# Two decoder blocks on one core: the first two split tiles behind each norm taken pair by pair, and a few steps of the mixers in another order

## Chip, cores and metric

The kernel runs on one NeuronCore of a Trainium2 chip. The metric is the device time of one execution in microseconds (us), taken as the median of several executions; lower is better. A difference of 0.2% (6.1 us) is about what can be told from no change.

## What is computed

An input x of 256 tokens and 1024 channels passes through two blocks. Cut to what matters:

```python
def first_block(x, ...):
    for i in range(2):
        h = rms_norm(x, norm_g[i, 0]) * (1.0 + sc1) + sh1
        x = x + g1 * (hgrn2_mixer(h, ...) if i % 2 == 0 else rglru_mixer(h, ...))
        h = rms_norm(x, norm_g[i, 1]) * (1.0 + sc2) + sh2
        x = x + g2 * peer_ffn(h, peer_w_q[i], ...)          # q = h @ w_q, then 16384 experts
    return rms_norm(x, final_g)

def second_block(x, ...):
    h = x
    for layer in range(2):
        mix = even_mixer(h, ...) if layer % 2 == 0 else odd_mixer(h, ...)   # start with h @ w_in
        h = layer_norm(ALPHA * h + mix, ...)
        ffn = conv_ffn(h, ffn_w_up[layer], ...)                             # starts with h @ w_up
        h = layer_norm(ALPHA * h + ffn, ...)
    return h
```

`even_mixer` runs a gated delta rule over 6 heads beside a dilated attention; `odd_mixer` runs a differential attention beside gated linear attention (GLA, `gla_chunked`), whose two normed outputs go through `w_out`. All is float32.

## The kernel before, in words

Activations are held transposed: 8 chunks of 128 channels by 256 tokens. Weights come as one long stream of tiles of 128x1024 (512 KB) through a ring of four buffers in SBUF, loaded by the queue of SyncE in the order of use. For most of them a product in full float32 is replaced by three passes in float32r: ScalarE rounds a tile to `w_high` (`split_high`, L1205, in two halves of 128x512), VectorE subtracts to get `w_low` (`split_low`, L2229, two halves too), and TensorE adds h_high*w_low, h_low*w_high and h_high*w_high (`passes`, L535 to L537). `w_high` and `w_low` have room for two tiles. A tile gives one chunk of 128 output channels and takes 8 input chunks, so 24 matmuls of 256 columns; its sums stand in one of four slots of PSUM (`product_slot`), and semaphores count its first half (`mid_tile`), its whole (`tile_done`) and the reading out of its slot (`product_taken`).

Each engine has its own program, and the order of work is written out by hand; only the choice of experts follows a table made ahead. Six of these products stand right behind a norm, so that their input is made while TensorE waits: `wq0` and `wq1` (queries of the two expert layers, behind an RMS norm with modulation), `even_in`, `up0`, `odd_in` and `up1`. There VectorE first scales the eight chunks by the inverse root (L1887, L1890), then ScalarE applies gain and shift twice for each chunk (`affine`: L1308 writes the rounded `h_high`, L1309 the whole value), and for each pair of chunks VectorE subtracts (`split_pair`, L1895), which makes `h_low` and raises `h_split` by one. So the input comes in four pairs of chunks. TensorE runs 12 idle matmuls of constants (`stay_busy`, L601: float32, so that each stands as two in the trace), waits for pair 0, takes its 6 matmuls of the first tile, runs 2 idle matmuls, waits for pair 1, and so on; from the second tile on nothing is waited for but weights:

```python
for q in range(4):
    m = 4 * b + q
    if fresh is not None and m % 2 == 0:
        stay_busy(busy[m // 2])
        pe.wait_ge(sem("h_split"), fresh[m // 2])
    ins = passes(dst, k, b, q, ...)
```

In `even_mixer` small steps stand between the 42 tiles of `even_in`, each behind tile j: `mixing` (L843, 12 columns at a time) behind 0, `beta_rows` (L853) behind 3, 5 idle matmuls and `gam_columns` (L862) behind 4, `gam_row` (L873) behind 5 to 7, attention from 9 on, and at the end 6 idle matmuls and `gdn_squares(0)` (L652) behind 38, `gdn_values` (L935) behind 39, `gdn_squares(1)` behind 40. ScalarE reads out tile j, rounds tile j + 2 and then does its small steps: the rows of beta (L1532) at j = 4, SiLU of q and k (L1549) and v (L1551) and the squares (L1265) at j = 36 to 38. In `odd_mixer` the projection of the gate (L1101, then L1108) stands behind tiles 0 and 1. GLA begins with transposes of v (L693), which ScalarE copies out (L1337) behind three other steps (squares, SiLU, rounding of two tiles); TensorE's second set of scores (L718) waits for that copy behind 8 idle matmuls.

Of the kernel before, what the change touches and what calls it, by code (L numbers as in the profile page):

```python
# [26 lines left out]
T = 256  # L27
# [173 lines left out]
def build(nc, tiles, ada_in, x_in, params_in, consts_in, small_in, masks_in, lam_in, bias_in, skew, out):  # L201
# [5 lines left out]
    with ctx:  # L207
# [277 lines left out]
        def _(pe):  # L485
# [65 lines left out]

# [6 lines left out]
            NORMED, MIXED = (12, 2, 2, 2), (0, 0, 0, 0)  # L558

            def split_linear(name, order=(0, 1, 2, 3), busy=MIXED):  # L560
# [4 lines left out]
                def body(k, it):  # L565
                    pe.wait_ge(taken, it * 4 + (q0 + k - 3))
                    split_product(product_slot(q0 + k), s0 + k, it, 4, h0 if k == 0 else None, busy)

                spans(pe, body, (0, 1, n) if any(busy) else (0, n))
# [175 lines left out]
            def peer(layer):  # L745
                split_linear(f"wq{layer}", busy=NORMED)
# [85 lines left out]
            def even_mixer():  # L832
# [105 lines left out]
                for j in range(n):  # L938
                    pe.wait_ge(taken, q0 + j - 3)
                    split_product(product_slot(q0 + j), s0 + j, 0, 4, h0 if j == 0 else None, NORMED)  # L940
# [115 lines left out]
            def odd_mixer():  # L1056
# [39 lines left out]
                for j in range(n):  # L1096
                    pe.wait_ge(taken, q0 + j - 3)
                    split_product(product_slot(q0 + j), s0 + j, 0, 4, h0 if j == 0 else None, NORMED)
# [6 lines left out]
                    if j == 1:  # L1105
# [85 lines left out]
        def _(act):  # L1191
# [84 lines left out]
            def rms(name=None, run=None):  # L1276
                if name in SUMS:
                    copy_sums(name)
                for i in range(DC // 2):
# [303 lines left out]
            def odd_mixer():  # L1583
# [53 lines left out]
                act.wait_ge(sem("diff_out_taken"), 4 * TT)  # L1637
                squares(e["mix"][:, 0:4 * T], e["sq"][:, 0:4 * T], "head_squares")
# [1249 lines left out]
```

## Time and profile before

| | us |
|---|---|
| median of 3 executions | 3068.2 (3067.02 to 3068.53) |
| the profiled execution, its own time | 3065.36 |
| its span in the profile | 3063.6 |
| TensorE, matmuls | 2980.6 busy (97%) |
| TensorE, weight loads | 2720.8 busy (89%) |
| VectorE | 2234.2 busy (73%) |
| ScalarE | 1633.2 busy (53%) |
| GpSimd | 62.1 busy (2%) |
| mean granted TensorE clock | 0.991 of full speed |

PE is TensorE's matmul side, PEld its weight loads, DVE is VectorE, ACT ScalarE, POOL GpSimd, SP SyncE. An engine is busy while one of its instructions executes; matmuls are pipelined, so that one stands with about 280 ns where the next starts 118 ns later. Idle matmuls of `stay_busy` count as busy.

### The profile page before, as it was taken

To read this page: it belongs to the slowest core of one execution; us is meant where nothing else is said; L and a number is where in the kernel's file an instruction comes from. 1 tells how busy PE (TensorE), PEld (TensorE's weight loads), DVE (VectorE), ACT (ScalarE), POOL (GpSimd) and SP (SyncE) were. 2 spreads that over 40 slices of the span, in tenths; PEclk is the share of its full clock that TensorE was granted. 3 is DMA by queue.
4 is the path that set the end of the run, shared out by engine and by line. 5 is a ranking of instruction groups with operands and counts; after the bars stand their busy time and mean duration, and the time that the engine had idled before them with its cause. 6 is when DMAs were issued, how large, how long until landed. Compare 5 with 4: busy or idle time off the path is not lost.

```text
span 3063.6 us, 58305 instructions
## 1 busy us (share of the span) xinstructions
PE 2980.6 (97%) x19920; PEld 2720.8 (89%) x19920; DVE 2234.2 (73%) x4764; ACT 1633.2 (53%) x3372; POOL 62.1 (2%) x112
## 2 busy tenths in 40 slices
PE   7998999999999999999999999999999999999998
PEld 6888899999987778889999988888898999888996
DVE  5336499888779985649898877777486678765786
ACT  1112557778644443655777854444555258463674
POOL 3000000000001100000000000000000000000000
PEclk8999999999999999999999999999999999999999
DMA  9521455444468863445444445555442145432453
GB/s 389 193 89 40 140 186 166 152 162 142 157 241 308 309 212 112 156 145 186 163 155 159 145 162 188 188 189 187 140 138 83 38 165 177 160 119 89 148 175 117
DMA packets 137692, 503.14 MB, mean 164 GB/s; under 512 B 15312, under 2 KB 15440, under 8 KB 137264
## 3 DMA queue, kind: packets, MB, share of 16 engines
q1 hardware_dynamic: 122544, 445.63, 43.2%
q0 software_dynamic: 14976, 55.19, 5.0%
q8 instruction: 112, 1.84, 0.2%
q14 instruction: 60, 0.49, 0.0%
HBM read 498.65 MB, written 2.10 MB: 163 GB/s over the span
## 4 chain that ended last, share of the span: by engine, by line
PE 81%; DVE 5%; ACT 4%; issue 1%; DVEq 0%; ACTq 0%
PE PB L535 14%; PE PB L536 14%; PE PB L537 13%; PE PA L581 9%; PE PA L582 9%; PE PA L580 8%; PE PA L777 4%; PE PB L525 2%; DVE w_low L2229 2%; PE PA L992 1%; PE PA L1165 1%; PE PA L631 1%; PE PB L601 1%; DVE BIG L2255 1%; ACT h_high L1308 1%
## 5 line engine op out<-in xcount | busy, mean ns | idle before, releaser
L1205 ACT ACTIVATE w_high<-ring 128x512 fp32r<-128x512 f32 x1548 | 962.2, 630 | 847.6 <-PE PA L582 466.4
L2229 DVE TENSOR_TENSOR w_low<-ring,w_high 128x512 fp32r<-128x512 f32 x1548 | 1051.0, 691 | 429.7 <-ACT w_high L1205 414.1
L535 PE MATMUL PB<-h_high,w_low 128*128 128x256 f32 x3792 | 1083.8, 286 | 15.2 <-DVE h_low L1895 6.2
L536 PE MATMUL PB<-h_low,w_high 128*128 128x256 f32 x3792 | 1067.9, 282 | 0.0
L537 PE MATMUL PB<-h_high,w_high 128*128 128x256 f32 x3792 | 1066.1, 281 | 0.0
L535 PEld LDWEIGHTS PB<-h_high,w_low 128*128 128x128 f32 x3792 | 721.4, 190 | 32.4 <-DVE h_low L1895 14.7
L536 PEld LDWEIGHTS PB<-h_low,w_high 128*128 128x128 f32 x3792 | 715.6, 189 | 0.2
L537 PEld LDWEIGHTS PB<-h_high,w_high 128*128 128x128 f32 x3792 | 714.5, 188 | 0.0
L581 PE MATMUL PA<-w_high,a_low 128*128 128x512 f32 x1200 | 476.3, 397 | 0.0
L580 PE MATMUL PA<-w_low,a_high 128*128 128x512 f32 x1200 | 470.4, 392 | 4.3 <-DVE a_low L2238 3.6
L582 PE MATMUL PA<-w_high,a_high 128*128 128x512 f32 x1200 | 474.0, 395 | 0.0
L580 PEld LDWEIGHTS PA<-w_low,a_high 128*128 128x128 f32 x1200 | 225.4, 188 | 68.9 <-issue 8.2
L581 PEld LDWEIGHTS PA<-w_high,a_low 128*128 128x128 f32 x1200 | 224.9, 187 | 53.0
L582 PEld LDWEIGHTS PA<-w_high,a_high 128*128 128x128 f32 x1200 | 225.2, 188 | 49.4
L525 PE MATMUL PB<-H,ring 128*128 128x256 f32 x896 | 198.3, 384 | 1.7 <-ACT H L1309 1.7
L525 PEld LDWEIGHTS PB<-H,ring 128*128 128x128 f32 x896 | 173.0, 193 | 26.0 <-issue 1.8
L777 PE MATMUL PA<-onehot_b,onehot_a 128*128 128x128 f32 x1024 | 137.5, 277 | 2.9 <-issue 2.6
L2238 DVE TENSOR_TENSOR a_low<-BIG,a_high 128x256 fp32r<-128x256 f32 x300 | 127.7, 426 | 10.3
L777 PEld LDWEIGHTS PA<-onehot_b,onehot_a 128*128 128x128 f32 x1024 | 124.8, 191 | 6.7 <-issue 3.3
L1855 DVE SCALAR_TENSOR_TENSOR BIG<-BIG,coef 128x1024 f32<-128x1024 f32 (+1 forms) x80 | 102.5, 1282 | 16.8 <-DMA BIG<-ada 15.2
L1411 ACT ACTIVATE onehot_a<-inv,slots 128x128 f32<-128x128 f32 x256 | 110.9, 481 | 0.0
L2255 DVE SCALAR_TENSOR_TENSOR BIG<-PB,par,BIG 128x255 f32 (+3 forms) x176 | 84.5, 480 | 14.8 <-DVE BIG L2255 14.5
(334 smaller groups left out, 2704.1 us busy)
## 6 DMA issues: line engine op xcount, KB each, us to landing
ring<-tiles SPq DMA_DIRECT2D x842, 512.0 KB, 3.3
BIG<-ada POOLq DMA_DIRECT2D x96, 512.0 KB, 6.6
BIG<-skew POOLq DMA_DIRECT2D x4, 512.0 KB, 5.0
X<-x SPq DMA_DIRECT2D x1, 1024.0 KB, 5.8
skew<-BIG POOLq DMA_DIRECT2D x1, 1024.0 KB, 6.3
out<-X SPq DMA_DIRECT2D x4, 256.0 KB, 2.1
con<-consts SPq DMA_DIRECT2D x1, 911.0 KB, 8.8
BIG<-masks POOLq DMA_DIRECT2D x1, 768.0 KB, 6.7
```

The source lines that it names most:

```text
L525: ins = mm(product_slot(q0 + i), wt[:, k * P:(k + 1) * P], src[:, k * T:(k + 1) * T], start=k == 0, stop=k == DC - 1)
L535: mm(dst, lhs_l, high, start=start, stop=False, skip_group_check=True)
L536: mm(dst, lhs_h, low, start=False, stop=False, skip_group_check=True)
L537: return mm(dst, lhs_h, high, start=False, stop=stop, skip_group_check=True)
L580: mm(dst, high[:, own], w_l, start=first, stop=False, skip_group_check=True)
L581: mm(dst, low[:, own], w_h, start=False, stop=False, skip_group_check=True)
L582: ins = mm(dst, high[:, own], w_h, start=False, stop=last, skip_group_check=True)
L777: ins = mm(PA[:, (g % 4 * 4 + i) * P:(g % 4 * 4 + i + 1) * P], onehot_a[:, i * P:(i + 1) * P], onehot_b[:, i * P:(i + 1) * P], start=True, ...
L1205: fn(tile_half(w_high, s, b), ring[:, at:at + HALF], ACT.Identity).then_inc(sem("high_ready"), 1)
L2229: tt(tile_half(w_low, s, b), ring[:, at:at + HALF], tile_half(w_high, s, b).bitcast(F32), ALU.subtract).then_inc(sem("low_ready"), 1)
L2238: tt(pair(a_low, j), a, pair(a_high, j).bitcast(F32), ALU.subtract)\
L2255: stt(dst, product_slot(q0 + j)[:, 0:T - sh], wt[tap][:, bass.ds(it * 4 + j, 1)], dst, ALU.mult, ALU.add).then_inc((taken, sem("conv_step" ...
```

## The change

Behind each of the six norms the first two tiles are taken together by a new function, `fresh_two`: 12 idle matmuls, then for each pair of input chunks 6 matmuls of tile 0 and 6 of tile 1, in two PSUM slots. There are no idle matmuls between the pairs. `even_in`, `up0`, `odd_in` and `up1` go side by side; `wq0` and `wq1` take tile 1 one pair later. So that tile 1's weights are there in time, VectorE makes its `w_low` between pairs 1 and 2 in `wq0` and `wq1`, and in `even_in` both engines split tile 1 ahead of the norm.

```diff
-            def split_product(dst, k, it, step, fresh=None, busy=(0, 0, 0, 0)):
+            def split_product(dst, k, it, step, fresh=None):
...
-                            stay_busy(busy[m // 2])
...
+            SIDE_BY_SIDE = [(i, part) for part in range(DC // 2) for i in range(2)]
+            ONE_LATER = [(0, 0), (0, 1), (1, 0), (1, 1), (0, 2), (1, 2), (0, 3), (1, 3)]
+
+            def fresh_two(q, k, fresh, busy, sequence):
+
+                for i in range(2):
+                    if q + i >= 4:
+                        pe.wait_ge(taken, q + i - 3)
+                stay_busy(busy)
+                for i, part in sequence:
+                    b = part // 2
+                    if part % 2 == 0:
+                        pe.wait_ge(sem("low_ready"), 2 * (k + i) + b + 1)
+                    pe.wait_ge(sem("h_split"), fresh[part])
+                    for m in (2 * part, 2 * part + 1):
+                        ins = passes(product_slot(q + i), k + i, b, m % 4, h_high[:, m * T:(m + 1) * T],
+                                     h_low[:, m * T:(m + 1) * T], m == 0, m == DC - 1)
+                    if part % 2:
+                        ins.then_inc((sem("mid_tile"), tile_done)[b], 1)
...
-            NORMED, MIXED = (12, 2, 2, 2), (0, 0, 0, 0)
+            NORMED = 12
...
-                spans(pe, body, (0, 1, n) if any(busy) else (0, n))
+                if sequence:
+                    fresh_two(q0, s0, h0, NORMED, sequence)
+                spans(pe, body, (2, n) if sequence else (0, n))
...
-                split_linear(f"wq{layer}", busy=NORMED)
+                split_linear(f"wq{layer}", sequence=ONE_LATER)
...
-                split_linear(f"up{i}", busy=NORMED)
+                split_linear(f"up{i}", sequence=SIDE_BY_SIDE)
```

The rest moves steps. `mixing` and the gate's first product now stand behind tiles 0 and 1, the gate's second product behind tile 2 in place of tile 1, `gam_columns` behind tile 5 in place of tile 4 and without its 5 idle matmuls (VectorE's part moves with it), `gdn_values` behind tile 38 with 4 idle matmuls in place of 6, and `gdn_squares(0)` behind tile 39. In GLA ScalarE copies v out first:

```diff
-                    if j == 4:
-                        stay_busy(5, IDLE_EVEN)
+                    if j == 5:
                         gam_columns()
...
                     if j == n - 4:
                         pe.wait_ge(sem("attention_out_taken"), 4 * TT)
-                        stay_busy(6, IDLE_EVEN)
+                        stay_busy(4, IDLE_EVEN)
+                        gdn_values()
+                    if j == n - 3:
                         gdn_squares(0)
-                    if j == n - 3:
-                        gdn_values()
...
-            def decay_attention(cfg):
+            def decay_attention(cfg, beside=None):
                 n = cfg["heads"] * T
                 act.wait_ge(sem("decay_vt_psum"), w.up(sem("decay_vt_psum")))
                 fn(cfg["vt"], PA[:, 0:n], ACT.Identity).then_inc(sem("decay_vt_ready"), 1)
+                if beside is not None:
+                    beside()
...
                 if run is not None:
-                    split_whole(dst, "whole_ready")
-                    split_low(run, 1)
+                    for i in range(DC // 2):
+                        split_pair(dst, "whole_ready", i)
+                        if i == 1:
+                            split_low(run, 1)
```

TensorE at the head of `up0`, before: the idle matmuls (L601), the first pair of tile 0 (L535 to L537), the wait for the second. `w_low` and `w_high` are the halves of the weight tile, `h_high` and `h_low` of the input.

```order
L601 MATMUL PB<-con 128x256 x11
L535 MATMUL PB<-h_high,w_low 128x256 [waits h_split]
L536 MATMUL PB<-h_low,w_high 128x256
L537 MATMUL PB<-h_high,w_high 128x256
L535 MATMUL PB<-h_high,w_low 128x256
L536 MATMUL PB<-h_low,w_high 128x256
L537 MATMUL PB<-h_high,w_high 128x256
L601 MATMUL PB<-con 128x256 x2
L535 MATMUL PB<-h_high,w_low 128x256 [waits h_split]
```

And now, from the second chunk of tile 0 on:

```order
L535 MATMUL PB<-h_high,w_low 128x256
L536 MATMUL PB<-h_low,w_high 128x256
L537 MATMUL PB<-h_high,w_high 128x256
L535 MATMUL PB<-h_high,w_low 128x256 [waits h_split,low_ready]
L536 MATMUL PB<-h_low,w_high 128x256
L537 MATMUL PB<-h_high,w_high 128x256
L535 MATMUL PB<-h_high,w_low 128x256
L536 MATMUL PB<-h_low,w_high 128x256
L537 MATMUL PB<-h_high,w_high 128x256
L535 MATMUL PB<-h_high,w_low 128x256 [waits h_split]
```

Where the idle matmuls stood, the same pair is now taken with tile 1's weights, and the wait for the next pair stands behind 12 matmuls and not 6.

VectorE at the head of `wq0`, before (L1890 scales, L1895 makes `h_low` of a pair, L2229 `w_low` of half a tile):

```order
L1890 TENSOR_TENSOR BIG<-X,inv 128x512 [waits dve_step]
L1890 TENSOR_TENSOR BIG<-X,inv 128x512 x3
L1895 TENSOR_TENSOR h_low<-BIG,h_high 128x512 [waits whole_ready] x4
L2229 TENSOR_TENSOR w_low<-ring,w_high 128x512 [waits high_ready] x2
L183 UNCONDITIONAL_BRANCH
```

And now (32 to 34 lines further down in the file):

```order
L1922 TENSOR_TENSOR BIG<-X,inv 128x512 [waits dve_step]
L1922 TENSOR_TENSOR BIG<-X,inv 128x512 x3
L1927 TENSOR_TENSOR h_low<-BIG,h_high 128x512 [waits whole_ready] x2
L2263 TENSOR_TENSOR w_low<-ring,w_high 128x512 [waits high_ready] x2
L1927 TENSOR_TENSOR h_low<-BIG,h_high 128x512 [waits whole_ready] x2
```

Tile 1's two halves moved ahead of the last two pairs.

TensorE in `even_in` behind tile 4, before (L862 is `gam_columns`, and the last row starts tile 5):

```order
L537 MATMUL PB<-h_high,w_high 128x256
L601 MATMUL PA<-con 128x256 x5
L862 MATMUL PA<-BIG,con 128x6 [waits g_ready,beta_rows_taken]
L862 MATMUL PA<-BIG,con 128x6 x2
L535 MATMUL PB<-h_high,w_low 128x256 [waits low_ready,product_taken]
```

And now, behind tile 5 (L883 is `gam_columns`, L894 a `gam_row`, the last row starts tile 6):

```order
L537 MATMUL PB<-h_high,w_high 128x256
L883 MATMUL PA<-BIG,con 128x6 [waits g_ready,beta_rows_taken]
L883 MATMUL PA<-BIG,con 128x6 x2
L894 MATMUL PA<-con,BIG 128x128 x6
L535 MATMUL PB<-h_high,w_low 128x256 [waits low_ready,product_taken]
```

The idle matmuls are gone, and a whole tile stands between `beta_rows` being sent to ScalarE and the wait for its copy.

## Rows read from the trace of the kernel before

**Rows 1.** The page's first part: busy us of each engine.

```profile
PE 2980.6 (97%) x19920; PEld 2720.8 (89%) x19920; DVE 2234.2 (73%) x4764; ACT 1633.2 (53%) x3372; POOL 62.1 (2%) x112
```

**Rows 2.** Timeline, head of up0: start us, us, engine, line [idle before <-releaser].

```profile
2471.58 0.39 PE L535 MATMUL PB<-h_high,w_low 128*128 128x256 f32 x1 [0.80 <-DVE h_low L1895]
...
2472.39 1.02 PE L601 MATMUL PB<-con 128*128 128x256 f32 x4
...
2472.80 0.69 DVE L1895 TENSOR_TENSOR h_low<-X,h_high 128x512 fp32r<-128x512 f32 x1 [1.27 <-ACT X L1309]
...
2477.48 0.38 PE L535 MATMUL PB<-h_high,w_low 128*128 128x256 f32 x1
2477.94 0.28 PE L535 MATMUL PB<-h_high,w_low 128*128 128x256 f32 x1
2478.29 0.28 PE L535 MATMUL PB<-h_high,w_low 128*128 128x256 f32 x1
```

**Rows 3.** Timeline, head of wq0, in all engines.

```profile
317.69 0.62 ACT L1205 ACTIVATE w_high<-ring 128x512 fp32r<-128x512 f32 x1
...
322.67 0.38 PE L535 MATMUL PB<-h_high,w_low 128*128 128x256 f32 x1 [0.73 <-DVE h_low L1895]
...
323.89 0.69 DVE L1895 TENSOR_TENSOR h_low<-BIG,h_high 128x512 fp32r<-128x512 f32 x1 [1.27 <-ACT BIG L1309]
...
328.43 2.51 DVE L2229 TENSOR_TENSOR w_low<-ring,w_high 128x512 fp32r<-128x512 f32 x4
```

**Rows 4.** TensorE's idle before two rows (timeline), in hg_out and even_mixer.

```profile
289.46 0.36 PE L535 MATMUL PB<-h_high,w_low 128*128 128x256 f32 x1 [1.84 <-DVE BIG L1951]
...
2350.91 1.56 PE L601 MATMUL PB<-con 128*128 128x256 f32 x6 [1.63 <-ACT BIG L1508]
```

**Rows 5.** Stretches: us, PE busy (x), granted clock as a share, DMA share, GB/s.

```profile
290.60:294.00 3.40, 3.40 (x19) 0.51 0.03 7
...
2351.00:2354.00 3.00, 3.00 (x14) 1.00 0.00 0
2185.00:2188.30 3.30, 3.30 (x18) 0.51 0.78 273
```

**Rows 6.** Timeline, head of even_in.

```profile
2175.17 0.47 PE L535 MATMUL PB<-h_high,w_low 128*128 128x256 f32 x1
...
2175.68 0.69 DVE L1895 TENSOR_TENSOR h_low<-X,h_high 128x512 fp32r<-128x512 f32 x1 [0.91 <-ACT X L1309]
...
2180.77 3.64 PE L843 MATMUL PA<-SM,X 128*128 128x12 f32 x32
...
2184.26 0.36 PE L535 MATMUL PB<-h_high,w_low 128*128 128x256 f32 x1
```

**Rows 7.** Timeline, even_in behind tile 4.

```profile
2199.87 2.32 PE L601 MATMUL PA<-con 128*128 128x256 f32 x10
...
2201.39 1.44 ACT L1532 ACTIVATE BIG<-PA 128x1536 f32<-128x1536 f32 x1
...
2202.88 0.83 PE L862 MATMUL PA<-BIG,con 128*128 128x6 f32 x6 [0.69 <-ACT BIG L1532]
2203.57 0.37 PE L535 MATMUL PB<-h_high,w_low 128*128 128x256 f32 x1
```

**Rows 8.** Timeline, even_in behind tile 38.

```profile
2330.68 2.75 PE L601 MATMUL PA<-con 128*128 128x256 f32 x12
...
2331.14 1.48 ACT L1551 ACTIVATE BIG<-BIG 128x1536 f32<-128x1536 f32 x1
...
2334.04 2.86 PE L652 MATMUL PA<-BIG,con 128*128 128x256 f32 x12 [0.61 <-ACT BIG L1265]
...
2336.55 0.47 PE L535 MATMUL PB<-h_high,w_low 128*128 128x256 f32 x1
```

**Rows 9.** Timeline, start of GLA in odd_mixer.

```profile
2773.80 3.72 PE L601 MATMUL PA<-con 128*128 128x256 f32 x16
...
2777.88 1.26 PE L718 MATMUL PA<-BIG 64*128 64x128 f32 x16 [0.36 <-ACT BIG L1337]
```

More of the change, by code:

```diff
@@ L556, in fresh_pairs, with split_linear @@
                 return [h0 + order.index(i) + 1 for i in range(DC // 2)]
-            NORMED, MIXED = (12, 2, 2, 2), (0, 0, 0, 0)
-            def split_linear(name, order=(0, 1, 2, 3), busy=MIXED):
+            NORMED = 12
+            def split_linear(name, order=(0, 1, 2, 3), sequence=None):
                 s0, (q0, n) = SPLIT_AT[name][0], product_at[name]
@@ L566, in body @@
                     pe.wait_ge(taken, it * 4 + (q0 + k - 3))
-                    split_product(product_slot(q0 + k), s0 + k, it, 4, h0 if k == 0 else None, busy)
-                spans(pe, body, (0, 1, n) if any(busy) else (0, n))
+                    split_product(product_slot(q0 + k), s0 + k, it, 4, h0 if k == 0 else None)
+                if sequence:
+                    fresh_two(q0, s0, h0, NORMED, sequence)
+                spans(pe, body, (2, n) if sequence else (0, n))
             def split_sums(j, k, it, step, first=False, last=False):
@@ L938, in even_mixer @@
                 for j in range(n):
-                    pe.wait_ge(taken, q0 + j - 3)
-                    split_product(product_slot(q0 + j), s0 + j, 0, 4, h0 if j == 0 else None, NORMED)
+                    if j == 0:
+                        fresh_two(q0, s0, h0, NORMED, SIDE_BY_SIDE)
+                    if j >= 2:
+                        pe.wait_ge(taken, q0 + j - 3)
+                        split_product(product_slot(q0 + j), s0 + j, 0, 4)
                     if j == 0:
@@ L1096, in odd_mixer @@
                 for j in range(n):
-                    pe.wait_ge(taken, q0 + j - 3)
-                    split_product(product_slot(q0 + j), s0 + j, 0, 4, h0 if j == 0 else None, NORMED)
+                    if j == 0:
+                        fresh_two(q0, s0, h0, NORMED, SIDE_BY_SIDE)
+                    if j >= 2:
+                        pe.wait_ge(taken, q0 + j - 3)
+                        split_product(product_slot(q0 + j), s0 + j, 0, 4)
                     if j == 0:
@@ L1104, in odd_mixer @@
                         ins.then_inc(sem("gate_psum"), 1)
-                    if j == 1:
+                    if j == 2:
                         pe.wait_ge(sem("gd_ready"), w.up(sem("gd_ready")))
@@ L1274, in copy_sums, with rms @@
                 fn(TMP[:, 0:D], PA[:, 0:D], ACT.Identity).then_inc(sem("sums_copied"), 1)
-            def rms(name=None, run=None):
+            def rms(name=None, run=None, early=None):
                 if name in SUMS:
                     copy_sums(name)
+                if early is not None:
+                    split_high(early, 1)
                 for i in range(DC // 2):
@@ L1636, in odd_mixer, with beside @@
                             .then_inc(sem("gla_gate_ready"), 1)
-                act.wait_ge(sem("diff_out_taken"), 4 * TT)
-                squares(e["mix"][:, 0:4 * T], e["sq"][:, 0:4 * T], "head_squares")
-                act.wait_ge(taken, q0 + n)
-                fn(e["r"], e["r"], ACT.Silu).then_inc(sem("gate_silu"), 1)
-                split_high("odd_out", 0)
-                split_high("odd_out", 1)
-                decay_attention(GLA)
+                def beside():
+                    act.wait_ge(sem("diff_out_taken"), 4 * TT)
+                    squares(e["mix"][:, 0:4 * T], e["sq"][:, 0:4 * T], "head_squares")
+                    act.wait_ge(taken, q0 + n)
+                    fn(e["r"], e["r"], ACT.Silu).then_inc(sem("gate_silu"), 1)
+                    split_high("odd_out", 0)
+                    split_high("odd_out", 1)
+                decay_attention(GLA, beside)
                 decayed_squares(e["sq"][:, 4 * T:8 * T], GLA_HEADS)
@@ L1727, in _ @@
             split_high("even_in", 0)
-            rms("experts1")
-            split_high("even_in", 1)
+            rms("experts1", early="even_in")
             affine(X, p("final_g"), None, "x_out", split=True)
@@ L2384, in even_mixer @@
                         gates()
-                    if j == 4:
+                    if j == 5:
                         gam_columns()
@@ L2674, in _ @@
             split_low("even_in", 0)
+            split_low("even_in", 1)
             rms("experts1", X)
             split_x()
-            split_low("even_in", 1)
             even_mixer()
```

## Prediction, made before the changed kernel was run

> **What bounds the kernel now.** I read the page's first part, then the timelines of the places that the change touches, then the granted clock of single stretches. TensorE is busy for 2980.6 of 3063.6 us and VectorE for 2234.2 [rows 1]: TensorE sets the pace, and what is taken out of its program shortens the run, if the others can follow. But busy counts idle matmuls too, so the page hides the time in question. The head of `up0` shows it [rows 2]. Pair 0 starts at 2471.58 and the last of the four at 2477.48, 5.90 us later: a pair comes every 1.97 us. Its 6 matmuls need 0.81 us (0.46 for the first chunk behind float32 work, then 0.35 for each chunk); 1.02 us more are idle matmuls, and then TensorE waits. What it waits for is made by ScalarE: VectorE sat idle for 1.27 us before `h_low`, released by ScalarE's L1309. So ScalarE sets 1.97 us for a pair, and TensorE uses two fifths of it. Meanwhile tile 1 is ready and waits for its turn. The same pattern stands in `wq0` [rows 3], `wq1`, `odd_in` and `up1`, with 1.96 to 1.97 us for a pair in each.
>
> **The change part by part.**
>
> *Five heads of this pattern.* A chunk costs 0.353 us (2477.94 to 2478.29), a tile of 8 chunks 2.82 us. Before, from the start of the last pair to the end of tile 1: 0.81 + 2.82 = 3.63 us. Now only the last pair of both tiles is left: 0.81 + 0.71 = 1.52 us. The gain is 2.11 us, the six chunks of tile 1 that now lie in the waits. Two pairs of work (1.52) fit in 1.97 us. The six idle matmuls that go cost nothing: they lay in the waits. In `wq0` and `wq1` VectorE has to put tile 1's two halves between pairs 1 and 2. Four halves took 2.51 us, so two take 1.25, and its gap there is 1.27 us [rows 3]: it fits with nothing to spare, and if it did not, pairs 2 and 3 would come some 0.1 us late. ScalarE has rounded tile 1 before pair 0 [rows 3]. Taking tile 1 one pair later leaves TensorE a gap of 1.97 - 0.81 = 1.16 us behind pair 0; then three pairs of work (0.81 + 0.71 + 0.71 = 2.23 us) run 0.26 us into pair 2, whose 1.41 us end before pair 3. What follows is late for nothing: tile 2 needs its first `w_low` half 1.5 us behind the last pair, and VectorE has that much less to do there, since tile 1 is behind it; its second half waits for tile 0's end, which stays where it was. Each head is worth 2.11 us, five are worth 10.6. In `odd_in` the gate's two products are moved and not changed. Bounds for one head: 0 if the waits only move to tile 2, 2.4 at most.
>
> *Head of `even_in`.* Here TensorE comes late: it starts pair 0 at 2175.17, while the last `h_low` is done at 2176.4 [rows 6]. So all pairs are ready, and the six idle matmuls are paid for. Before, tile 0 and its idle matmuls took 5.60 us (to 2180.77). Now both tiles take 16 chunks, 5.65 us, and 0.19 for the slow first one: 5.84. `mixing` (3.49 us) follows, and tile 2 starts 0.24 us behind the point where tile 1 started. A tile of 2.82 + 0.10 is gone, for 0.24: 2.7 us. The two splits moved ahead of the norm lie beside adds and squares, and TensorE has 12 idle matmuls of cover behind them; if they delayed the norm by their 1.3 us, pair 0 would still be there in time. Behind `mixing` the clock is 0.51 for 3.3 us [rows 5]. Its place behind `mixing` stays, so I leave this cost (1.65 us) as it is: it would now fall on tile 2.
>
> *`gam_columns`.* From the end of tile 4 to tile 5 it took 3.70 us (2199.87 to 2203.57): 2.32 idle matmuls, 0.69 waiting for ScalarE's copy of the beta rows, 0.69 its own [rows 7]. The copy ended at 2202.83, 2.96 us behind tile 4. Tile 5 now covers 2.82 of that, so 0.2 us of wait and the 0.69 stay: 2.8 us gained. VectorE's part moves with it; the rows of decay that follow it are needed a tile later, and ScalarE's next rounding (tile 7) stands behind the copy, 4 us before TensorE needs it. Bounds: 0 (the wait moves to the first `gam_row`) and 3.0.
>
> *Tail of `even_in`.* Before, 3.36 us passed from 2330.68 to the start of the squares, with 0.61 idle for ScalarE. The transposes of v need only its SiLU, done at 2331.14 + 1.48 = 2332.62, and the 4 idle matmuls end at 2332.5 [rows 8]. So they start 2.0 us behind tile 38, and the squares find their input done a tile later. The root that follows still waits for the last squares. Gain 1.4 us; bounds 0.5 (the two idle matmuls alone) and 1.5.
>
> *GLA.* The scores waited 0.36 us more than their 3.72 us of idle matmuls [rows 9]. The copy comes out 3 us earlier, the idle matmuls stay: 0.4 us. What ScalarE did before the copy has the whole of the scores' loop as cover. Bounds 0 and 0.4, since nothing shortens the idle matmuls.
>
> Sum: 10.6 + 2.7 + 2.8 + 1.4 + 0.4 = 17.9 us. The profiled execution's 3065.4 would become 3047.5; the median lies 2.8 us above it, so 3068.2 - 17.9 = **3050.3 us**.
>
> **Weighed against a rule.** The idle matmuls keep the clock. After 1.84 us without a matmul in `hg_out` [rows 4] the granted clock was 0.51, 1.2 GHz, from 290.6 for 3.4 us; after 1.63 us it stayed at 1.00, 2.4 GHz [rows 4, 5]. In `wq0` the new gaps are 0.73 and 1.16 us with 0.81 us of work between, 1.89 together, just in the range where it fell. The Trainium skill, TensorE: Matmul & The Clock Gate, section "Why this matters for your kernels", tells one only to avoid idle gaps of over about 3 us. By that rule no gap here matters and the sum stays 17.9 us; by the rows it can fall, and the trace differs from the rule, since 1.84 us were enough.
>
> **The rivals.**
>
> *The clock falls in `wq0` or `wq1`.* For it: the rows above. Against: two gaps are not one, and in the other four heads the gap between pairs is only 0.45 us, less than the waits that the clock stands now. Price: from pair 1 on there are 14 chunks, which end 5.5 us later. With 3.4 us at half clock, 4.8 chunks are done there and 9.2 (3.2 us) left: 6.6 us, so 1.2 lost. One head gives 3051.5, both 3052.7 us.
>
> *`even_in` gives back what it gains at `gam_columns`.* There ScalarE and VectorE work in a fixed order, and copy, columns and decay rows now come closer together. For it: ScalarE's copy already ended last [rows 7]. Without the 2.8 us: 3053.1 us; without the tail's 1.4 as well, 3054.5.
>
> *The slow stretch behind `mixing` goes.* 48 dense matmuls stand before it now. 1.7 us less: 3048.6 us.
>
> *The change doesn't do what it says.* Two tiles in turn, each with its own slot, could run slower than one, or the waits could all come back at tiles 2 and 3. Without the 10.6 and the 2.7 us: 3063.6 us. Against it: the weights of all tiles are ready well ahead in the trace, and each chunk loads new weights anyway.
>
> *Slower.* The idle matmuls between pairs go in all six heads. If the clock fell there and stayed down, each 3.4 us at half costs 1.7 us where TensorE doesn't wait. The point from which it decides is 17.9 / 1.7, 11 such stretches. At three for each head, 18 x 1.7 = 30.6 us, it would be 3080.9 us. Against it: between pairs TensorE works 1.52 of 1.97 us.
>
> **How the numbers follow.** Forecast 50%, clock 25%, `even_in` 13%, slow stretch gone 5%, not as it says 5%, slower 2%. The likeliest is 3050.3 us. The range takes in the first four cases, with 1.5 us for the runs' own spread at the lower end: 3047.0 to 3055.0 us. Only the last two cases and some tails lie outside. Faster by over 0.2% (6.1 us, about what a measurement can tell): 0.93; within 0.2%: 0.05; slower: 0.02.
>
> **What would show it.** Right: in `up0` four starts of a pair 1.97 us apart, 12 matmuls behind each, tile 2 about 1.5 us behind the last; in `wq0` VectorE's L1895, L1895, two `w_low` and L1895 with no delay of the third; in `even_in` tile 2 starting at the distance at which tile 1 did, no idle before `gam_columns` over 0.3 us, and `gdn_values` 2.0 us behind tile 38. Wrong: a clock of 0.5 in any of the six heads, idle time of TensorE at tiles 2 or 3 released by `w_low`, or a wait for the decay rows behind tile 6. A gain of under 13 us would mean that one of the larger terms failed.

## The result, and the profile after

| | before | changed |
|---|---|---|
| median, us | 3067.6 (3065.0 to 3068.5, 4 executions) | 3049.2 (3048.1 to 3050.1, 4 executions) |
| ratio, 95% interval | | 0.9941 (0.9924 to 0.9958) |
| span of the profiled execution | 3063.6 | 3048.4 |
| mean granted clock of TensorE | 0.991 | 0.990 |

The change makes the kernel 18.4 us faster by the medians; the interval of the ratio allows 13 to 23. The forecast was 3050.3 us. A later set of five executions (e4 below) gave 3048.0 against 3065.5 for the kernel before on the same chip, 17.5 us less. TensorE's line of the page, which answers to [rows 1], hardly shows it: its busy time fell by 14.4 us, with 86 matmuls fewer, and it is still at 97%.

```profile
PE 2966.2 (97%) x19834; PEld 2712.9 (89%) x19834; DVE 2232.6 (73%) x4764; ACT 1631.9 (54%) x3372; POOL 62.3 (2%) x112
```

So one has to read distances. The table takes, in each trace, the distance in us between two steps of TensorE that both kernels have: from the squares ahead of a norm to the next step named. e4 is the changed kernel, profiled a second time.

| stretch of TensorE | before | changed | e4 | gain | forecast |
|---|---|---|---|---|---|
| wq0: squares to the first step of the experts | 58.19 | 57.20 | 56.08 | 0.99, in e4 2.11 | 2.11 |
| wq1: the same | 58.27 | 56.17 | 56.17 | 2.10 | 2.11 |
| even_in: squares to `mixing` | 18.48 | 18.73 | 18.73 | -0.25 | -0.24 |
| even_in: `mixing` to the first `gam_row` | 25.72 | 20.02 | 19.98 | 5.70 | 5.7 |
| from there to the squares ahead of up0 | 255.39 | 254.02 | 254.06 | 1.37 | 1.4 |
| up0, to the next squares | 212.27 | 210.13 | 210.71 | 2.14, in e4 1.56 | 2.11 |
| odd_in with its mixer and GLA | 162.51 | 159.76 | 159.76 | 2.75 | 2.5 |
| up1, to the next squares | 213.57 | 211.41 | 211.46 | 2.16 | 2.11 |

(The forecast's 2.7 us for the head of even_in are the -0.24 and 2.92 of the 5.7.) The changed column adds up to 17.0 us, e4's to 17.5. Why up0 gave 0.6 less in e4: most of it begins at 2479.82, where TensorE waits 0.27 us for a half of `w_low`: VectorE took 1.8 us for each of two halves beside steps of GpSimd, and takes 0.69 for one elsewhere. That GpSimd is the cause isn't shown.

The span fell by 15.2 only, because the code that both share didn't take the same time in the two executions: from the first squares of the program to those of wq0 it took 301.8 us in place of 299.9 (in the other profiles below 299.7 to 302.0). Slow stretches, in which the granted clock is at its lower level, stand in other places too: the one of before at 382.8 is absent, and others stand at 217.8 and 1371.5. In the same way 1.4 of the 18.4 us by which the medians differ stand in no row of the table. That is why the runs spread over 3 us, and why single terms are read from distances and not from spans.

Timeline of the changed kernel, head of `up0` (start us, us, engine, line, [idle before <-releaser]); it answers to [rows 2]:

```profile
2463.54 0.36 PE L535 MATMUL PB<-h_high,w_low 128*128 128x256 f32 x1 [0.90 <-DVE h_low L1927]
...
2464.67 0.69 DVE L1927 TENSOR_TENSOR h_low<-X,h_high 128x512 fp32r<-128x512 f32 x1 [1.27 <-ACT X L1337]
2465.42 0.39 PE L535 MATMUL PB<-h_high,w_low 128*128 128x256 f32 x1 [0.22 <-DVE h_low L1927]
...
2467.48 0.36 PE L535 MATMUL PB<-h_high,w_low 128*128 128x256 f32 x1 [0.38 <-DVE h_low L1927]
...
2469.36 0.39 PE L535 MATMUL PB<-h_high,w_low 128*128 128x256 f32 x1 [0.23 <-DVE h_low L1927]
```

The pairs still come 1.9 to 2.1 us apart (2463.54, 2465.42, 2467.48, 2469.36), and VectorE still waits 1.27 us for ScalarE's whole value. But between them stand four chunks of work, and TensorE waits only 0.2 to 0.4 us.

The same view of VectorE in `wq0` answers to [rows 3]. The columns are the same.

```profile
325.82 0.69 DVE L1927 TENSOR_TENSOR h_low<-BIG,h_high 128x512 fp32r<-128x512 f32 x1 [1.28 <-ACT BIG L1337]
326.43 1.29 DVE L2263 TENSOR_TENSOR w_low<-ring,w_high 128x512 fp32r<-128x512 f32 x2
327.80 0.69 DVE L1927 TENSOR_TENSOR h_low<-BIG,h_high 128x512 fp32r<-128x512 f32 x1
329.76 0.69 DVE L1927 TENSOR_TENSOR h_low<-BIG,h_high 128x512 fp32r<-128x512 f32 x1 [1.27 <-ACT BIG L1337]
```

The two halves of tile 1 fill the gap exactly: pair 2 comes at 327.80, 1.98 us behind pair 1, and pair 3 again 1.96 later. TensorE and its granted clock (stretch, us, PE busy, clock as a share, DMA share, GB/s) in `wq0`, `wq1` and behind `mixing`:

```profile
324.70:326.50 1.80, 0.94 (x6) 1.00 0.00 0
326.90:330.30 3.40, 3.40 (x19) 0.52 0.40 131
1316.40:1319.80 3.40, 3.39 (x29) 1.00 0.44 134
2183.20:2186.60 3.40, 3.40 (x20) 0.60 0.94 340
```

In `wq0` the granted clock is 0.52 over 3.4 us, which is its lower level of 1.2 GHz for all but the start, behind two waits of 0.82 and 0.92 us with 0.9 us of work between them: 19 matmuls in 3.4 us. In `wq1`, the same program with waits of 0.91 and 0.93 us, it stayed at 1.00 (2.4 GHz), with 29. The slow stretch behind `mixing` is there as before [rows 5]. The move of `gam_columns` and the tail of even_in answer to [rows 7] and [rows 8]:

```profile
2197.53 1.45 ACT L1562 ACTIVATE BIG<-PA 128x1536 f32<-128x1536 f32 x1
2199.03 0.83 PE L883 MATMUL PA<-BIG,con 128*128 128x6 f32 x6
...
2323.96 1.89 PE L622 MATMUL PA<-con 128*128 128x256 f32 x8
2324.43 1.48 ACT L1581 ACTIVATE BIG<-BIG 128x1536 f32<-128x1536 f32 x1
2325.96 1.53 PE L956 MATMUL PA<-con,BIG 128*128 128x128 f32 x12
```

ScalarE's copy ends at 2198.98, while tile 5 runs, and `gam_columns` follows with no wait. `gdn_values` starts 2.0 us behind tile 38. In GLA the second set of scores follows its idle matmuls directly (2764.86, where it waited 0.36 us [rows 9]).

### The profile page after: what moved, and what is told of

The parts are those of the page before. It is cut to its first block, busy times and chain, and to the rows that moved or that the text cites. A ratio compares the mean times of both kernels' runs of the same rounds, so it can differ in the third digit from the quotient of the medians.

```text
span 3048.4 us, 58151 instructions
## 1 busy us (share of the span) xinstructions
PE 2966.2 (97%) x19834; PEld 2712.9 (89%) x19834; DVE 2232.6 (73%) x4764; ACT 1631.9 (54%) x3372; POOL 62.3 (2%) x112
## 4 chain that ended last, share of the span: by engine, by line
PE 81%; DVE 5%; ACT 3%; issue 1%; DVEq 0%; ACTq 0%
PE PB L535 14%; PE PB L536 14%; PE PB L537 13%; PE PA L602 9%; PE PA L603 9%; PE PA L601 9%; PE PA L798 4%; PE PB L525 2%; DVE w_low L2263 2%; PE PA L1015 1%; PE PA L1191 1%; PE PA L652 1%; DVE BIG L2289 1%; PE PB L622 1%; ACT h_high L1336 1%
## 5 line engine op out<-in xcount | busy, mean ns | idle before, releaser
L535 PE MATMUL PB<-h_high,w_low 128*128 128x256 f32 x3792 | 1084.1, 286 | 18.1 <-DVE h_low L1927 11.0
L537 PE MATMUL PB<-h_high,w_high 128*128 128x256 f32 x3792 | 1067.7, 282 | 0.0
L535 PEld LDWEIGHTS PB<-h_high,w_low 128*128 128x128 f32 x3792 | 723.2, 191 | 31.1 <-issue 15.7
L537 PEld LDWEIGHTS PB<-h_high,w_high 128*128 128x128 f32 x3792 | 716.1, 189 | 0.0
L601 PE MATMUL PA<-w_low,a_high 128*128 128x512 f32 x1200 | 471.4, 393 | 4.3 <-DVE a_low L2272 3.5
L601 PEld LDWEIGHTS PA<-w_low,a_high 128*128 128x128 f32 x1200 | 226.0, 188 | 68.8 <-issue 8.2
```

What stands on the lines that cost most here:

```text
L535: mm(dst, lhs_l, high, start=start, stop=False, skip_group_check=True)
L537: return mm(dst, lhs_h, high, start=False, stop=stop, skip_group_check=True)
L601: mm(dst, high[:, own], w_l, start=first, stop=False, skip_group_check=True)
```

## Experiments

Each was timed in four or five executions (e1 in eleven), beside the kernel before on the same chip: its median was 3065.5 us beside e1 to e4, 3067.2 beside e5 to e8, 3067.0 beside e9 to e11 and 3065.8 beside e12. e4 was timed beside the first of these, so that differences to e4 in e5 to e12 hold the difference between chips too; where it matters, the gain over each one's own before is given beside them. Medians of the same kernel differ by up to 1.7 us here. So for a term of a few us the distances in the trace decide, and the time only bounds it.

**e4, the changed kernel again.** No edit.

> The changed kernel unchanged, as the base of the three others on the same chip and as a second look at wq0. Theory (the fall of the clock in wq0 comes from its two gaps of 0.8 and 0.9 us and is there in each execution): 3049.2 us, and again a stretch near 0.5 behind pair 1 of wq0, none in wq1. Rival (chance of where in time the gaps fall): the fall is absent here, or stands in wq1.

Measured: 3048.0 us, ratio 0.9941 (0.9927 to 0.9954). The same head of `wq0`, with the same waits, at full clock:

```profile
322.88 0.36 PE L535 MATMUL PB<-h_high,w_low 128*128 128x256 f32 x1 [0.83 <-DVE h_low L1927]
324.75 0.39 PE L535 MATMUL PB<-h_high,w_low 128*128 128x256 f32 x1 [0.93 <-DVE h_low L1927]
```

```profile
325.10:328.50 3.40, 3.40 (x30) 1.00 0.42 139
```

The distance of wq0 is 56.08 us, 1.12 less than with the fall. The fall is therefore no fixed property of this program: the rival holds in that it was absent. That it is chance isn't shown by this; e11 comes back to it. The price of the fall is 1.12 us.

**e1, the kernel before without the idle matmuls between pairs.** This asks whether the gain is in taking tile 1 along, or in the idle matmuls that went.

```diff
-            NORMED, MIXED = (12, 2, 2, 2), (0, 0, 0, 0)
+            NORMED, MIXED = (12, 0, 0, 0), (0, 0, 0, 0)
```

> The kernel before, with the 2 idle matmuls between pairs taken out in all six heads (the 12 ahead of pair 0 stay). Nothing else. Theory (the heads gained because tile 1's chunks fill waits; the idle matmuls lay in those waits and cost nothing, but for even_in, where TensorE came late and paid 6 x 0.41 = 2.5 us for them): about 2.5 us faster than before, 3065.1 us, and in up0 still four pairs 1.97 us apart with 1.1 us idle ahead of each. Rival A (the idle matmuls themselves were the cost in every head): 10 to 18 us faster, 3050 to 3057 us. Rival B (without idle matmuls the granted clock falls where the waits are 1.1 us of each 1.97): slower, by up to 1.2 us for each of the five heads.

Measured: 3071.4 us, ratio 1.0019 (1.0010 to 1.0028): 5.9 us **slower** than before. TensorE in `wq0`, and then its clock in wq0, wq1, up0, odd_in and up1 behind the third pair:

```profile
324.61 0.39 PE L535 MATMUL PB<-h_high,w_low 128*128 128x256 f32 x1 [0.74 <-DVE h_low L1895]
326.58 0.48 PE L535 MATMUL PB<-h_high,w_low 128*128 128x256 f32 x1 [1.00 <-DVE h_low L1895]
```

```profile
328.70:332.10 3.40, 3.14 (x13) 0.50 0.03 5
1322.10:1325.50 3.40, 3.15 (x13) 0.50 0.00 0
2477.70:2481.00 3.30, 2.37 (x18) 1.00 0.08 20
2690.20:2693.60 3.40, 3.14 (x13) 0.50 0.00 0
2854.60:2858.00 3.40, 3.14 (x14) 0.50 0.02 5
```

The clock fell in four of the five heads. By distances the five cost 1.36, 1.31, 0.23 (up0, where it held though the waits between its pairs were 0.93 to 1.08 us), 1.65 and 1.42 us more than before, and the head of even_in 2.58 less, as forecast: together 3.4 us slower. (The stretch behind the first experts took 1.6 us more: this profile has a further 3.1 us in slow stretches there, and the 1.5 at 382.8 of before are absent.) So Rival B, though four of its heads cost more than its 1.2 us, with Theory right only for even_in. The idle matmuls lay in waits and cost nothing, but they were not idle in effect: they kept the clock. The change could drop them only since tile 1's matmuls took their place.

**e2, the heads alone.** `gam_columns`, the tail and GLA's copy are back as before.

```diff
-                    if j == 5:
+                    if j == 4:
+                        stay_busy(5, IDLE_EVEN)
                         gam_columns()
...
-                        stay_busy(4, IDLE_EVEN)
-                        gdn_values()
+                        stay_busy(6, IDLE_EVEN)
+                        gdn_squares(0)
...
-                decay_attention(GLA, beside)
+                beside()
+                decay_attention(GLA)
```

> The changed kernel with gam_columns, the tail of even_in (gdn_squares, gdn_values) and GLA's copy put back as before, idle matmuls too: only the six heads are changed. Theory: the ledger of the traces gives the mixer's moves 2.9 + 1.4 + 0.4 = 4.7 us, so 3053.9 us, and behind tile 4 the wait of 0.7 us for ScalarE's L1558 copy is back. Rival (the moves only shifted waits, and the heads made it all): 3049 to 3050 us. Rival (the moves are worth more than the traces' stretches show, since the medians differ by 18.4 us and the traces by 15.2): 3056 us or more.

Measured: 3052.7 us, 4.7 more than e4. By distances against e4: `mixing` to `gam_row` 22.89 (+2.91), tail 255.40 (+1.34), odd_in with its mixer 160.19 (+0.43), together 4.68. The wait is back, to the hundredth the one of [rows 7]:

```profile
2193.12 2.32 PE L622 MATMUL PA<-con 128*128 128x256 f32 x10
...
2194.64 1.44 ACT L1563 ACTIVATE BIG<-PA 128x1536 f32<-128x1536 f32 x1
2196.13 0.83 PE L883 MATMUL PA<-BIG,con 128*128 128x6 f32 x6 [0.69 <-ACT BIG L1563]
```

**e3, wq0 and wq1 as they were.** One tile in pairs with idle matmuls between, VectorE's split behind the last pair.

```diff
-                if sequence:
+                two = sequence is SIDE_BY_SIDE
+                if two:
                     fresh_two(q0, s0, h0, NORMED, sequence)
-                spans(pe, body, (2, n) if sequence else (0, n))
+                spans(pe, body, (2, n) if two else (0, 1, n) if sequence else (0, n))
...
-                        if i == 1:
+                        if i == DC // 2 - 1:
                             split_low(run, 1)
```

> The changed kernel with wq0 and wq1 as they were: one tile in pairs with 2 idle matmuls between them, VectorE's second split behind the last pair. Theory (2.11 us for each head, whatever the clock does): 4.2 us slower than the changed kernel, 3053.4 us. Rival (in wq the gain is given back by the granted clock, which was 0.67 behind pair 1 in wq0's profile): 2.0 to 3.1 us slower only, and no stretch at 0.5 in wq0 here.

Measured: 3052.9 us, 4.9 more than e4. From the squares, wq0 took 2.11 and wq1 2.12 us more than in e4, and no slow stretch stands in either head. 2.11 us a head is right; where the clock falls, as in the first profile, half of it is given back.

**e6, `gam_columns` behind tile 4 without idle matmuls.**

```diff
-                    if j == 5:
+                    if j == 4:
                         gam_columns()
```

(the same on VectorE)

> The changed kernel with gam_columns back behind tile 4 (VectorE's part too), but without the 5 idle matmuls. Theory (the gain of 2.9 us came from tile 5 lying over ScalarE's copy, not from the idle matmuls being gone): TensorE waits 3.0 us for L1558 behind tile 4 and the run is 2.9 us slower than the changed kernel; if a wait of 3 us lowers the granted clock, 4.5 us slower. Rival (the idle matmuls were what cost the time): no slower than the changed kernel.

Measured: 3052.0 us, 4.0 more than e4 (its gain over its own before is 15.2 us, 2.3 less than e4's); `mixing` to `gam_row` takes 24.10 us (+4.12). TensorE and ScalarE, then the clock behind it:

```profile
2195.14 1.44 ACT L1562 ACTIVATE BIG<-PA 128x1536 f32<-128x1536 f32 x1
2196.63 0.83 PE L883 MATMUL PA<-BIG,con 128*128 128x6 f32 x6 [2.85 <-ACT BIG L1562]
```

```profile
2199.00:2201.40 2.40, 2.40 (x13) 0.50 0.03 9
```

The 2.9 us of the move are back, and 1.2 more for a clock that fell behind a wait of 2.85 us. The gain came from the tile that covers the copy, not from the idle matmuls being gone.

**e8, wq0 and wq1 side by side.**

```diff
-                split_linear(f"wq{layer}", sequence=ONE_LATER)
+                split_linear(f"wq{layer}", sequence=SIDE_BY_SIDE)
```

> The changed kernel with wq0 and wq1 side by side too, in place of one pair later; VectorE's order as it is, so tile 1's first w_low half comes behind pair 1. TensorE then waits in front of tile 1's pair 0, 1.65 us (from 325.5 to 327.15 in the changed profile's times) and does all the rest behind it. Theory (the last pair sets the end either way, the order in between only moves waits): 0.15 us slower for each head, 0.3 in all, if the granted clock holds, and up to 1.2 us more for each head where it falls. Rival (one pair later is what makes the gain in wq): 2 us slower for each head, 4 in all, with the clock at 1.00.

Measured: 3049.4 us, which time alone can't tell from e4. The distances are 57.57 and 57.67 us, 1.49 and 1.50 more than e4's. TensorE waited 1.53 and 1.52 us for tile 1's `w_low`, and the clock behind it, in wq0 and wq1, was at its lower level:

```profile
326.20:328.60 2.40, 2.40 (x13) 0.50 0.48 125
1316.00:1318.40 2.40, 2.40 (x13) 0.50 0.44 125
```

The theory's terms add up roughly (0.15 and up to 1.2 for a head), and the rival's 2 us for a head at full clock do not. Like with like, a head of this order with the clock fallen against a head of ONE_LATER with it fallen (57.20 in wq0, 57.29 in wq1, by e12), side by side costs 0.37 and 0.38 us more. Whether the clock also falls more often side by side isn't shown by these two heads; e11 says why.

**e11, idle matmuls in wq's two waits.**

```diff
+                    stay_busy(between.get((i, part), 0))
...
-                    fresh_two(q0, s0, h0, NORMED, sequence)
+                    fresh_two(q0, s0, h0, NORMED, sequence, {(0, 1): 2, (1, 0): 1} if sequence is ONE_LATER else {})
```

> The changed kernel with idle matmuls in wq's two larger waits: 2 ahead of tile 0's pair 1, 1 ahead of tile 1's pair 0. They end before the input is there (0.8 of 1.16 us, 0.4 of 0.7 us). So far the granted clock fell in 3 of 10 such heads in the profiles of this order (changed kernel and its neighbours), at 1.1 us each. Theory (the waits bring it about): granted clock 1.00 in both heads here, and 0 to 1 us faster than the changed kernel, too little for the times. Rival (the waits have no part in it): a stretch near 0.5 here too.

Measured: 3047.7 us; distances 56.09 and 56.20 us, the full gain in both. wq0's head and its granted clock:

```profile
325.60 1.02 PE L623 MATMUL PB<-con 128*128 128x256 f32 x4
327.49 0.59 PE L623 MATMUL PB<-con 128*128 128x256 f32 x2
```

```profile
325.20:328.60 3.40, 3.34 (x23) 1.00 0.02 5
1313.70:1317.10 3.40, 3.33 (x23) 1.00 0.00 0
```

Counted over all profiles, with two heads each: with the waits of the change the clock fell in 5 of 12 heads (the changed kernel, e2, e4, e5, e6, e12), side by side in 2 of 2, and in none of 8 where the second wait is filled (e11) or only 0.4 us long (e7, e9 and e10 below); the wait of 0.8 to 0.9 us ahead of pair 0 stays in all of them. The expectation's "3 of 10" was the count ahead of e12, which added two.

The falls are not scattered over these heads. Ahead of each of the five that fell, the clock had also fallen once 34 to 38 us earlier, and ahead of none of the seven that held. For wq0 that earlier place is behind the wait of 1.84 us in `hg_out` [rows 4], which stands in every profile; for wq1 it is behind 32 matmuls of one column, at about 1278 us. The place ahead of wq0 in the changed kernel, e4 and e11, and that ahead of wq1 in e12:

```profile
292.90:296.30 3.40, 3.40 (x19) 0.50 0.03 7
291.10:294.50 3.40, 3.38 (x29) 1.00 0.02 5
292.60:296.00 3.40, 3.40 (x18) 0.50 0.03 7
1278.90:1282.30 3.40, 3.40 (x11) 0.50 0.00 0
```

The two side-by-side heads of e8 have such an earlier fall as well, so they show no more than that the clock falls there too. Of the eight heads without the second long wait, four have it: wq0 in e7, e10 and e11, and wq1 in e9. None of them fell, nor did wq0 of before and of e3, which have it too and idle matmuls between their pairs. So among the heads with an earlier fall it is five of five with the waits of the change and none of six without, which speaks for the waits as a condition of the fall; e11's wq1, with no fall ahead of it, says little. What links the two falls isn't shown, and an earlier fall isn't needed everywhere: in e1 the clock fell in odd_in and up1 with none ahead of them.

**e5, fewer idle matmuls ahead of even_in.** In the changed profile pair 0 stood ready by 2170.3 and TensorE came at 2173.85.

```diff
-                        fresh_two(q0, s0, h0, NORMED, SIDE_BY_SIDE)
+                        fresh_two(q0, s0, h0, 4, SIDE_BY_SIDE)
```

> The changed kernel with 4 idle matmuls ahead of pair 0 of even_in in place of 12. In the changed profile pair 0's h_low is made by 2170.3 us and the last by 2175.0, while the idle matmuls hold TensorE until 2173.85, and both tiles end at 2179.70. Theory (the head of even_in is bound by TensorE's own idle matmuls, and would next be bound by the last pair, 2175.04 + 1.5 = 2176.6): mixing starts 3.1 us earlier and the run is 3.1 us faster than the changed kernel. Rival A (what follows waits instead: mixing for ScalarE's copy of the bias rows, tile 2 for w_low): 0 to 1.5 us. Rival B (the 0.2 us waits between pairs, with the idle time around, lower the granted clock once more): 1.4 us.

Measured: 3043.9 us, ratio 0.9924 (0.9911 to 0.9938), 4.1 less than e4 by the medians (over its own before it gains 23.4 us, 5.9 more than e4, so the time alone gives 4 to 6). The squares-to-`mixing` distance is 15.67 us, 3.06 less than e4's 18.73. The bound is now the last pair: VectorE's last `h_low` ends at 2174.10, and `mixing` starts 1.58 us behind it.

```profile
2173.41 0.69 DVE L1927 TENSOR_TENSOR h_low<-X,h_high 128x512 fp32r<-128x512 f32 x1 [0.91 <-ACT X L1337]
2175.68 3.64 PE L864 MATMUL PA<-SM,X 128*128 128x12 f32 x32
```

**e7, one of ScalarE's four steps for a pair given to VectorE.**

```diff
-                        fn(h_high[:, m * T:(m + 1) * T], dk, ACT.Identity, scale=g, **add)
-                    ins = fn(dk, dk, ACT.Identity, scale=g, **add)
+                        ins = fn(h_high[:, m * T:(m + 1) * T], dk, ACT.Identity, scale=g, **add)
+                    if not split or m % 2 == 0:
+                        ins = fn(dk, dk, ACT.Identity, scale=g, **add)
...
+                    m = 2 * i + 1
+                    dk = src[:, m * T:(m + 1) * T]
...
+                        ins = v.tensor_scalar(dk, dk, gain[:, m:m + 1], shift[:, m:m + 1], ALU.mult, ALU.add)
```

> The changed kernel with one of ScalarE's four steps for a pair given to VectorE: the whole value of each odd chunk (in place, before h_low is subtracted). Same computation. Theory (ScalarE's four steps of 0.49 us set the pair's 1.97 us, as the prediction said): pairs come 1.48 us apart in up0, odd_in, up1, the last one 1.5 us earlier, TensorE's wait between pairs goes from 0.4 to 0.1 us; 1.4 us for each of these three and 1.0 to 1.4 in wq0 and wq1, where VectorE's split of tile 1 is in the way; nothing in even_in, where TensorE comes late: 6 to 7 us faster than the changed kernel, 3042 us. Rival A (VectorE, with its wait on its own step, becomes the bound: pair at 1.6 to 1.8 us): 2 to 4 us faster. Rival B (ScalarE was not the pace): no gain.

Measured: 3042.3 us, ratio 0.9918 (0.9905 to 0.9932), 5.7 less than e4 (24.9 less than its own before, 7.4 more than e4's gain). In up0 VectorE's `h_low` comes every 1.42 to 1.49 us, and TensorE takes the four pairs with no wait of 0.2 us or more between them:

```profile
2458.97 0.69 DVE L1937 TENSOR_TENSOR h_low<-X,h_high 128x512 fp32r<-128x512 f32 x1
2459.95 0.41 DVE L1934 TENSOR_SCALAR X<-X,par 128x256 f32<-128x256 f32 x1 [0.28 <-ACT h_high L1336]
2460.39 0.69 DVE L1937 TENSOR_TENSOR h_low<-X,h_high 128x512 fp32r<-128x512 f32 x1
```

```profile
2459.80:2466.00 6.20, 6.19 (x52) 1.00 0.15 48
```

So ScalarE did set the pace. By distances against e4, up0, odd_in and up1 lost 2.0, 1.47 and 2.29 us. 1.4 of each lie in the head. The rest of up0 is mostly e4's own wait at 2479.82, since against the changed kernel's first profile up0 lost 1.42; the rest of up1 I didn't follow. The profile also lacks the slow stretch behind `mixing` (1.5 us), for which the edit gives no reason. wq0 and wq1 lost only 0.74 and 0.73, less than the 1.0 to 1.4 expected. There the split of tile 1 makes VectorE the bound: its next four steps follow one another without a gap.

```profile
324.51 1.28 DVE L2271 TENSOR_TENSOR w_low<-ring,w_high 128x512 fp32r<-128x512 f32 x2
325.72 0.41 DVE L1934 TENSOR_SCALAR BIG<-BIG,coef,mod 128x256 f32<-128x256 f32 x1
326.16 0.69 DVE L1937 TENSOR_TENSOR h_low<-BIG,h_high 128x512 fp32r<-128x512 f32 x1
326.77 0.41 DVE L1934 TENSOR_SCALAR BIG<-BIG,coef,mod 128x256 f32<-128x256 f32 x1
327.21 0.69 DVE L1937 TENSOR_TENSOR h_low<-BIG,h_high 128x512 fp32r<-128x512 f32 x1
```

**e9, e5 and e7 together.** Both edits above.

> e5 and e7 together: 4 idle matmuls ahead of pair 0 of even_in, and VectorE makes the whole value of each odd chunk in all six heads. Theory (the two act in different places): 3.1 + 6.2 = 9.3 us faster than the changed kernel, 3039.5 us. Rival (in even_in the pairs come sooner too, but TensorE is bound there by its own 5.8 us of work, or VectorE's extra step delays the root's successors): 6 to 8 us.

Measured: 3037.6 us, ratio 0.9906 (0.9891 to 0.9921): 10.4 less than e4 by the medians (9.3 expected), 29.4 less than before on the same chip, where e4 has 17.5. It beats both kernels and is the version to keep.

**e10, e9 with `mixing` in two halves,** and **e12, that alone on the changed kernel.** In eleven of the twelve profiles with `mixing` in one piece a slow stretch followed it.

```diff
-                    if j == 0:
-                        mixing()
+                    if j in (0, 2):
+                        mixing(j // 2)
```

(VectorE's and ScalarE's steps on its result one tile later)

> e9, and the 32 matmuls of 12 columns of mixing stand in two halves, 16 behind tile 1 and 16 behind tile 2, what ScalarE and VectorE do with them one tile later. Theory (3.5 us of such matmuls in one piece are what the slow stretch of 1.65 us behind them follows from, seen behind mixing in the profiles of before and of the changed kernel): no stretch at 0.5 behind either half, 1.6 us faster than e9. Rival A (the stretch comes from something else, or from where in time it falls; it was absent in e7's profile): same time as e9. Rival B (what is one tile later on ScalarE, two loads of its tables, makes w_low late for tile 4 or 5): up to 1.5 us slower than e9.

> The changed kernel with mixing in two halves as in e10, and nothing else. e9 and e10 did not differ in time by what their spread can tell, but from the start of mixing to gam_columns e10's profile took 17.77 us and e9's 19.29, and had no slow stretch. Theory (the slow stretch follows the piece of 3.5 us of 12-column matmuls): none behind either half here, 1.5 us less in that part than in the changed kernel, time about 1.5 us below the changed kernel. Rival (chance: the stretch was absent in one of twelve profiles with mixing in one piece too, e7's): it may stand here, and then the part takes as long as before.

Measured: e10 3037.2 us, e12 3048.5 us. From `mixing` to `gam_columns` e10 took 17.77 us (e9 19.29) and e12 17.79 (the changed kernel 19.33). No slow stretch stands behind either half; e12:

```profile
2179.22 1.85 PE L865 MATMUL PA<-SM,X 128*128 128x12 f32 x16
2183.85 1.85 PE L865 MATMUL PA<-SM,X 128*128 128x12 f32 x16
```

```profile
2180.80:2184.20 3.40, 3.40 (x31) 1.00 0.57 128
2184.20:2187.60 3.40, 3.40 (x31) 1.00 1.03 389
```

1.5 us are gone in that place in both, as the theory had it, but neither median shows them: e10 is 0.4 us below e9, e12 0.5 above e4. That is inconclusive. In each profile the time went elsewhere: e12's has the clock low in wq0 and in wq1, 1.1 us each, and e10's took 3.0 us more than e9's from the experts of wq0 to the next squares (807.49 against 804.45), with slow stretches at 379.5 and 1164.6. Whether the halves make falls elsewhere more frequent, or this is spread, one profile of each kernel can't tell.

## Why the prediction was right

The time came out 1.1 us below the forecast, and the terms were right one by one, not only their sum. Luck has a share in how close it came: the distances give 17.0 us in the profile, in which a fall of the clock that the sum had left out cost 1.1, and the medians 18.4.

- **The five heads, 2.11 us each.** Measured 2.11 (wq0 in e4) and 2.10 (wq1), with 0.99 in wq0 where the clock fell; confirmed by undoing (e3, 2.11 and 2.12), 2.14 in up0 and 2.16 in up1; odd_in with GLA 2.75 where 2.51 were expected (by e2, 2.32 of it belong to the head). The mechanism was the one told: pairs 1.97 us apart by ScalarE, and six chunks of tile 1 in the waits. e7 confirmed the pace by changing it.
- **Head of even_in and `gam_columns`.** 5.45 us for 2.7 + 2.8. By e6 and e2, 2.9 belong to `gam_columns`, so 2.5 to the head. That is what e1's head gained from losing its six idle matmuls alone, 2.58: in even_in, TensorE came late and all its input was there, so the order of the tiles gave next to nothing. That the idle matmuls stand in front of ready input I saw, but I didn't ask of the 12 ahead of pair 0 what I asked of the 6 behind it; e5 found 3.1 us there.
- **Tail and GLA.** 1.37 for 1.4, and 0.43 for 0.4 (e2).
- **"The six idle matmuls that go cost nothing: they lay in the waits."** True of their time, and the weakest sentence of the prediction all the same. e1 shows that without them the clock falls in four of five heads, at 1.3 to 1.65 us. I had the granted clock as a cost of wq's new waits alone, and a cover of 1.52 us of work in each 1.97 elsewhere; it is this cover that made the sentence harmless: in up0, odd_in and up1 the clock fell in none of the 36 heads of the twelve profiles with the two tiles.
- **The clock in wq, rival at 25%.** It took place: in the first profile in wq0, and in 5 of 12 heads, at 1.12 us, where I had put 1.2. So one of the signs that I had named as showing the prediction wrong, a clock of 0.5 in a head, did appear, while the terms held. It is not a case that holds or doesn't, but a cost that comes in some executions: on average about 0.9 us for the two heads together, estimated from these profiles (5/12 x 1.12 x 2). The forecast should have carried that as a term.
- **The rule weighed.** The Trainium skill, TensorE: Matmul & The Clock Gate, section "Why this matters for your kernels", warns of idle gaps of over about 3 us. Here half the clock followed one wait of 2.85 us (e6), waits of 0.82 and 1.53 us with one pair of work between (e8), and waits of 0.82 and 0.92 us (the changed kernel). Behind the 1.84 us in `hg_out`, from which I had read that they were enough, it fell in 10 of the 14 profiles and held in e2, e4, e5 and e9. The measurement decides: waits shorter than the rule's can be followed by a fall, but not in each execution.
- **The other rivals.** even_in gave nothing back; the slow stretch behind `mixing` stayed (and is absent in e7, so that too isn't fixed); the change did what it said.

## What to carry to other kernels

Where an input arrives in pieces more slowly than one tile can use them, take two tiles side by side: the gain is the work of the second that fits into the waits, and it can be read off before (time between pieces, time of a tile's share of one). Find out who makes the pieces, since moving one of four steps to an engine with slack (e7) gave another 1.4 us in the heads of up0, odd_in and up1, and 0.7 in wq, where that engine had work of its own in the way. Idle matmuls have to be priced twice: by whether the input is already there, in which case they cost time (in e5, 3.06 us for eight of them, until the input set the bound), and by what the clock does without them (e1); take them out only where work takes their place.

## What was not expected of the hardware

- The same instructions with the same waits kept the clock in one execution and lost it in the next (wq0: 0.52 in the changed profile, 1.00 in e4). One profile can't say whether a head is safe; it took twelve heads to see five falls, and each of these stood behind another fall 34 to 38 us earlier, so that heads have to be compared with heads that share it.
- 48 dense matmuls ahead of `mixing` did not prevent the slow stretch behind it, while two halves of 1.85 us with a tile between had none (two profiles). The 32 matmuls of 12 columns count as busy on the page for their 3.64 us, and the clock fell behind them in 11 of 12 profiles all the same; the earlier fall ahead of wq1 begins 0.2 to 1.1 us behind 32 matmuls of one column (3.63 us), in 5 of 14.
